# The opening of a decoder layer, rearranged: three arrival signals for x, statistics by row tile, and a first GLA head that begins with its value projections

## Chip, cores and metric

One core of one Trainium2 chip. The metric is the device time of one execution in microseconds. The kernel before took 2632.35 us (median of three runs, 2630.19 to 2633.02).

## The reference

One layer of a hybrid decoder runs for 256 prompt rows and 8 sample rows, which share all weights (264 columns in the kernel, where activations stand transposed). Only its first part matters here:

```python
h = rmsnorm(x, norm_mix_pre)              # x: 256 + 8 rows of 2048
z = h @ w_in                              # columns: pool, dilated q/k/v, then
gq, gk, gv, gr, ga, gates = ...           # GLA: 4 heads of q 256, k 256, v 512, r 512; ga 16 wide
log_a = log_sigmoid(ga @ gla_w_a2 + gla_b_a) / 16
b = cumsum(log_a, within chunks of 64)
q_t, k_t, k_h = q * exp(b), k * exp(-b), k * exp(b_last - b)
A = tril(q_t @ k_t.T); o = A @ v + q_t @ S     # S: state carried from chunk to chunk
y_gla = rmsnorm(o) * gla_norm * silu(gr)
```

After it come the dilated attention, the pooling branch, the merge, cross-attention and the ConvFFN; the change leaves these alone.

## The kernel before

Every weight matrix is read once, in slots of 128 columns by 2048 rows (1 MB). SP issues a slot's load into one of three raw buffers (`load`). ACT writes a rounded copy `weights_hi` in two halves (`split_hi`), DVE the rest `weights_lo = raw - hi` (`split_lo`). PE multiplies a slot with the activations in 16 blocks of three matmuls of 264 columns (`product`: hi by hi, hi by lo, lo by hi), 48 in all, into bank 0, 1 or 2, and the bank is emptied by ACT or DVE. Semaphores count slots and banks: the split of slot c+3 is made after the product of slot c.

The order of work is the order in which each engine's program is written, with waits on counting semaphores; nothing reorders it. POOL first gives every semaphore its starting credits (`credits`), then makes the identity and other constants. ACT's queue issues 17 loads of parameters, SP's queue the two 1 MB tiles of x (128 rows each) and the 8 sample rows, all under one semaphore `x_loaded`; the first weight load waits for it as well.

When all of x is there (L2142 to L2154 on DVE, L994 to L1000 on ACT) the sums of squares of all rows, one square root and one reciprocal for three columns of statistics, and the scaling follow. PE meanwhile turns the parameter rows and makes the attention bias products (L1553 to L1562). Then PE turns x, 128 columns at a time: three transposes (`turn`, L587) give one column tile of 264. ACT writes its `h_hi` (L1010) and DVE its `h_lo` (L2170), from banks 3 to 7 in turn. From the sixth tile on, each round of three transposes is followed by one block (three matmuls) of the first slot, the one that holds ga (`gate_block`, phase `PH_GA`). The text below calls this a round. Five blocks are left when the last tile is turned.

Then ga goes to SBUF, PE makes eight gate sums (`ga @ gla_w_a2`, L1694, 16 rows deep), DVE adds the bias (L2182), ACT and DVE make the log decay and its running sums for head 0 (`log_decay(0)`), and ACT the exponentials. `gla_head` runs 12 slots per head, in the order q0 q1 k0 k1, v0 to v3, r0 to r3. Between slots PE does the small products of the chunked form: `t_kh` (turn k) after slot 4, `a` (scores) after 5, `t_v` (turn v) after 8, `s0` after 9 and `s1` after 10. Head 0 is written out; heads 1 to 3 are a loop, in which `gla_tail` adds the sample rows' work of the head before. The emptying of the q banks multiplies by the exponentials, so it waits for them; the emptying of the v banks (ACT, L1062) is a copy.

## Time and profile before

| | |
|---|---|
| median of three runs | 2632.35 us (2630.19 to 2633.02) |
| span of the profiled execution, first to last instruction | 2631.0 us |
| mean granted TensorE clock | 0.993 |
| busy: PE, DVE, ACT, POOL | 98%, 61%, 48%, 7% |
| DMA | 530.96 MB, mean 202 GB/s |

The profiled execution's own time is not listed apart from the runs; its span stands 1.35 us under their median. PEclk is the granted TensorE clock as a part of 2.4 GHz: 1.00 is the level of 2.4 GHz, 0.50 that of 1.2 GHz. Idle time stands in brackets behind a row, with what ended it.

### The profile page before, as it was taken

What the parts mean: (1) busy time and instruction counts of PE and PEld (TensorE: products, weight loads), DVE (VectorE), ACT (ScalarE), POOL (GpSimd) and SP (SyncE); (2) the same over time, 40 slices, a digit from 0 to 9 for tenths busy, and PEclk for the clock granted to TensorE, in tenths of its full rate; (3) what the DMA queues carried; (4) which work ended last, traced back from release to release, by engine and by line L of the source; (5) the groups of instructions that cost most, each with busy time, mean ns of one, the idle gap of its engine ahead of it and who ended that gap; (6) DMA issues with size and microseconds to landing.
All of it is one profiled execution on the core that took longest, in us unless ns stands there. A gap on an engine that the chain in (4) does not pass through costs nothing. (4 is left out here: it accounts for less than half of the span.)

```text
span 2631.0 us, 53824 instructions
## 1 busy us (share of the span) xinstructions
PE 2567.6 (98%) x20841; PEld 2479.6 (94%) x20841; DVE 1601.4 (61%) x2439; ACT 1254.7 (48%) x1948; POOL 195.7 (7%) x307
## 2 busy tenths in 40 slices
PE   7999999999999999999999999998999999999997
PEld 5988988999999999999999998987999999999997
DVE  4556565544565556555654656546777765777766
ACT  5455555433444444443444644435554554554553
POOL 1112111000111111100000001500000000000000
PEclk9999999999999999999999999999999999999999
DMA  6688789667888888866666747954566567666563
GB/s 202 207 266 272 240 254 297 176 180 209 238 233 232 233 232 230 222 193 192 168 178 207 207 131 208 310 172 129 160 176 182 156 187 194 184 184 175 162 186 107
DMA packets 855053, 530.96 MB, mean 202 GB/s; under 512 B 13961, under 2 KB 832065, under 8 KB 854135
## 3 DMA queue, kind: packets, MB, share of 16 engines
q1 hardware_dynamic: 822583, 440.07, 60.8%
q0 software_dynamic: 27312, 86.50, 9.5%
q10 hardware_dynamic: 5032, 2.62, 0.4%
q8 instruction: 91, 1.49, 0.2%
q14 instruction: 35, 0.29, 0.0%
HBM read 499.79 MB, written 33.29 MB: 203 GB/s over the span
## 5 line engine op out<-in xcount | busy, mean ns | idle before, releaser
L572 PE MATMUL bank<-h_hi,weights_hi 128*128 128x264 f32 x4624 | 1338.7, 290 | 16.2 <-DVE h_lo L2767 7.0
L545 DVE TENSOR_TENSOR weights_lo<-weights_raw,weights_hi 128x1024 fp32r<-128x1024 f32 x814 | 959.5, 1221 | 611.3 <-ACT weights_hi L537 611.1
L573 PE MATMUL bank<-h_lo,weights_hi 128*128 128x264 f32 x4624 | 1317.9, 285 | 0.0
L574 PE MATMUL bank<-h_hi,weights_lo 128*128 128x264 f32 x4624 | 1316.8, 285 | 0.0
L572 PEld LDWEIGHTS bank<-h_hi,weights_hi 128*128 128x128 f32 x4624 | 877.3, 190 | 41.9 <-issue 24.4
L537 ACT ACTIVATE weights_hi<-weights_raw 128x1024 fp32r<-128x1024 f32 x814 | 813.7, 1050 | 204.3 <-PE bank L574 196.5
L573 PEld LDWEIGHTS bank<-h_lo,weights_hi 128*128 128x128 f32 x4624 | 878.4, 190 | 2.1 <-issue 1.9
L574 PEld LDWEIGHTS bank<-h_hi,weights_lo 128*128 128x128 f32 x4624 | 873.9, 189 | 0.0
L572 PE MATMUL bank<-y_hi,weights_hi 128*128 128x264 f32 x1232 | 351.7, 285 | 5.0 <-DVE weights_lo L545 2.6
L574 PE MATMUL bank<-y_hi,weights_lo 128*128 128x264 f32 x1232 | 350.3, 284 | 0.0
L573 PE MATMUL bank<-y_lo,weights_hi 128*128 128x264 f32 x1232 | 348.8, 283 | 0.0
L572 PEld LDWEIGHTS bank<-y_hi,weights_hi 128*128 128x128 f32 x1232 | 232.1, 188 | 6.0 <-issue 3.0
L574 PEld LDWEIGHTS bank<-y_hi,weights_lo 128*128 128x128 f32 x1232 | 232.3, 189 | 0.0
L573 PEld LDWEIGHTS bank<-y_lo,weights_hi 128*128 128x128 f32 x1232 | 232.2, 189 | 0.0
L1148 ACT ACTIVATE qkv<-bank 128x264 f32<-128x264 f32 x72 | 28.1, 390 | 256.2 <-PE bank L574 252.4
L2797 DVE TENSOR_TENSOR squares<-bank,rstd 128x264 f32<-128x264 f32 x88 | 38.0, 432 | 81.4 <-PE bank L574 76.6
L1148 ACT ACTIVATE y_hi<-ffn_value 128x264 f32 (+1 forms) x44 | 18.7, 425 | 140.3 <-DVE ffn_value L2815 140.3
L572 PE MATMUL bank<-memory_normed_hi,weights_hi 128*128 128x256 f32 x256 | 76.5, 299 | 0.0
L573 PE MATMUL bank<-memory_normed_lo,weights_hi 128*128 128x256 f32 x256 | 72.2, 282 | 0.0
L574 PE MATMUL bank<-memory_normed_hi,weights_lo 128*128 128x256 f32 x256 | 71.7, 280 | 0.0
L1499 ACT ACTIVATE ffn_value<-squares,parameters 128x264 f32<-128x264 f32 x44 | 26.7, 608 | 79.8 <-DVE squares L2797 79.8
L964 POOL DMA_DIRECT2D out_conv_p<-conv_new_rows x1 | 0.8, 781 | 842.0 <-DVE conv_new_rows L2859 842.0
(406 smaller groups left out, 2193.9 us busy)
## 6 DMA issues: line engine op xcount, KB each, us to landing
weights_raw<-in_w_in SPq DMA_DIRECT2D x177, 1024.0 KB, 7.0
weights_raw<-in_w_up SPq DMA_DIRECT2D x88, 1024.0 KB, 5.6
weights_raw<-in_w_down SPq DMA_DIRECT2D x64, 704.0 KB, 4.9
gla_state_sample<-in_state_gla POOLq DMA_DIRECT2D x32, 512.0 KB, 8.5
out_gla_s<-gla_state_sample POOLq DMA_DIRECT2D x32, 512.0 KB, 6.2
weights_raw<-in_w_br_gla SPq DMA_DIRECT2D x16, 1024.0 KB, 6.1
weights_raw<-in_w_mix_out SPq DMA_DIRECT2D x16, 1024.0 KB, 6.2
weights_raw<-in_w_xkv SPq DMA_DIRECT2D x16, 1024.0 KB, 6.7
```

The costliest lines, as they stand in the source:

```text
L537: nc.scalar.activation(w_hi[:, r, half], raw[:, r, half], ACT.Copy).then_inc(hi_ready, 1)
L545: nc.vector.tensor_tensor(w_lo[:, r, half], raw[:, r, half], w_hi[:, r, half].bitcast(F32), ALU.subtract).then_inc(lo_ready, 1)
L572: nc.tensor.matmul(out, wh, xh, start=first and n == 0, stop=False)
L573: nc.tensor.matmul(out, wh, xl, start=False, stop=False)
L574: mm = nc.tensor.matmul(out, wl, xh, start=False, stop=last and n == len(blocks) - 1)
L964: pool.dma_start(A["conv_p"][0, 0].rearrange("r (t p) -> t r p", p=P), newtok[:, 0:2, :]).then_inc(conv_out, 16)
L1148: return nc.scalar.activation(out, in_, ACT.Copy)
L1499: nc.scalar.activation(c, sqr[:, j % 3, :], ACT.Identity, scale=param(PC_CW + 176 + col, n), bias=param(PC_CB + col, n)).then_inc(S(f"c{j} ...
L2797: nc.vector.tensor_tensor(u, bank[p.outs[j]][:, 0:T], rstd[:, :], ALU.mult).then_inc(evac[p.outs[j]], 1)
```

## The change

- SP loads the sample rows first, then the two tiles of x, each under its own semaphore; nine small parameter loads and w_a2 move from ACT's queue to SP's, behind x. ACT's queue begins with the bias inputs.
- POOL gives credits to the four setup counters first and clears the statistics before it makes the identity; the other credits come behind the constants.
- The statistics go by part: sample rows, first tile, second tile (its two column halves squared by ACT and DVE side by side). The second tile is scaled in four quarters, and the turning may begin after the first of them. The parameter copy moves from DVE to ACT.
- PE makes the bias products before it turns the parameters.
- From the tenth round on each round has a second block, of slot v0 of head 0. Head 0 runs v0 to v3, q0 q1 k0 k1, r0 to r3 (`FIRST_HEAD`): four gate sums before slot v1 and four behind it, `t_kh` after the ninth slot, `a` and `t_v` after the tenth, `s0` after the eleventh, `s1` after the twelfth. Heads 1 to 3 keep their order (`HEAD`).

The core of the diff (a line of "..." where lines are left out):

```diff
+        QK = [("q", 0), ("q", 1), ("k", 0), ("k", 1)]
+        VS = [("v", t) for t in range(4)]
+        RS = [("r", t) for t in range(4)]
+        class HeadOrder:
+            def __init__(self, kinds, t_kh, a, qx, t_v, s0, s1, o0, o1):
+                self.kinds, self.t_kh, self.a, self.qx, self.t_v = kinds, t_kh, a, qx, t_v
+                self.s0, self.s1, self.o0, self.o1 = s0, s1, o0, o1
+                self.at = {kind: j for j, kind in enumerate(kinds)}
+        HEAD = HeadOrder(QK + VS + RS, t_kh=4, a=5, qx=6, t_v=8, s0=9, s1=10, o0=10, o1=11)
+        FIRST_HEAD = HeadOrder(VS + QK + RS, t_kh=8, a=9, qx=9, t_v=9, s0=10, s1=11, o0=11, o1=11)
+        FIRST_SPLITS = [2, 7, 12]
...
@@ -623,17 +647,25 @@
         @block.sync
         def _(sp):
+            sp.dma_start(xtok_s[:, :], A["x_sample"][:, 0, :]).then_inc(xs_loaded, 16)
             for m in range(2):
-                sp.dma_start(xtok[:, m, :], A["x_prompt"][0, m * P:(m + 1) * P, :]).then_inc(x_loaded, 16)
-            sp.dma_start(xtok_s[:, :], A["x_sample"][:, 0, :]).then_inc(x_loaded, 16)
-            sp.wait_ge(x_loaded, 48)
+                sp.dma_start(xtok[:, m, :], A["x_prompt"][0, m * P:(m + 1) * P, :]).then_inc(x_loaded[m], 16)
+            for name, r0 in PARAMS:
+                src = A[name].rearrange("l (t p) -> (l t) p", p=P)
+                sp.dma_start(prow[r0:r0 + src.shape[0], 0, :], src).then_inc(par_loaded, 16)
+            sp.dma_start(w_a2[:, :], A["gla_w_a2"][0]).then_inc(a2_loaded, 16)
+            sp.wait_ge(x_loaded[0], 16)
+            sp.wait_ge(x_loaded[1], 16)
             load(sp, PH_GA, 0, 0, w_cols(COL_GA))
-            with sp.Fori(0, 4) as h:
-                for j in range(12):
-                    kind, t = [("q", 0), ("q", 1), ("k", 0), ("k", 1)][j] if j < 4 else ("vr"[j // 8], j % 4)
+            def gla_loads(h, order):
+                for j, (kind, t) in enumerate(order.kinds):
                     col = {"q": h * 256 + COL_GQ, "k": h * 256 + COL_GK, "v": h * 512 + COL_GV,
                            "r": h * 512 + COL_GR}[kind]
                     load(sp, PH_GLA, j, h, w_cols(col + t * P))
+            gla_loads(0, FIRST_HEAD)
+            with sp.Fori(1, 4) as h:
+                gla_loads(h, HEAD)
...
-            for s, n in credits:
+            for s, n in first_credits:
                 pool.sem_inc(s, n)
+            nc.gpsimd.memset(stat[:, 0:13], 1.0).then_inc(G_SET("stat1"), 1)
+            nc.gpsimd.memset(stat[:, 13:14], D * EPS).then_inc(G_SET("stat"), 1)
...
-            nc.gpsimd.memset(stat[:, :], 1.0).then_inc(G_SET("stat"), 1)
+            for s, n in credits:
+                pool.sem_inc(s, n)
             nc.gpsimd.memset(scan_keep[:, :], 1.0).then_inc(G_SET("keep1"), 1)
             pool.wait_ge(*G_SET.at("keep1"))
@@ -969,48 +1004,46 @@
         @block.scalar
...
-            act.wait_ge(x_loaded, 48)
+            act.wait_ge(xs_loaded, 16)
             act.wait_ge(*G_SET.at("stat"))
-            ours = ((0, xtok[:, 0, :], P), (2, xtok_s[:, :], NS))
-            for m, x, n in ours:
-                if m:
-                    act.wait_ge(*A_SET.at("sq0"))
-                nc.scalar.activation(junk[0][0:n, :], x, ACT.Square, accum_out=stat[0:n, m:m + 1])\
-                    .then_inc(A_SET(f"sq{m}"), 1)
-            act.wait_ge(*V_SET.at("var"))
-            nc.scalar.activation(stat[:, 6:9], stat[:, 3:6], ACT.Sqrt).then_inc(A_SET("root"), 1)
-            act.wait_ge(*V_SET.at("rstd"))
-            for m, x, n in ours:
-                nc.scalar.activation(x, x, ACT.Copy, scale=stat[0:n, 9 + m:10 + m]).then_inc(A_SET(f"sx{m}"), 1)
+            nc.scalar.activation(junk[0][0:NS, :], xtok_s[:, :], ACT.Square, accum_out=stat[0:NS, 2:3])\
+                .then_inc(A_SET("sq2"), 1)
+            act.wait_ge(*V_SET.at("var2"))
+            nc.scalar.activation(stat[:, 8:9], stat[:, 5:6], ACT.Sqrt).then_inc(A_SET("root2"), 1)
+            act.wait_ge(x_loaded[0], 16)
+            act.wait_ge(*A_SET.at("sq2"))
+            nc.scalar.activation(junk[0][:, :], xtok[:, 0, :], ACT.Square, accum_out=stat[:, 0:1]).then_inc(A_SET("sq0"), 1)
+            act.wait_ge(*V_SET.at("var0"))
+            nc.scalar.activation(stat[:, 6:7], stat[:, 3:4], ACT.Sqrt).then_inc(A_SET("root0"), 1)
+            act.wait_ge(x_loaded[1], 16)
+            act.wait_ge(*A_SET.at("sq0"))
+            nc.scalar.activation(junk[0][:, 0:D // 2], xtok[:, 1, 0:D // 2], ACT.Square, accum_out=stat[:, 12:13])\
+                .then_inc(A_SET("sq1"), 1)
+            act.wait_ge(*V_SET.at("ss1"))
+            nc.scalar.activation(stat[:, 7:8], stat[:, 4:5], ACT.Sqrt, scale=1.0 / D).then_inc(A_SET("root1"), 1)
+            act.wait_ge(*P_SET.at("par"))
+            nc.scalar.activation(par[:, 0:PC_END], bank[6][:, 0:PC_END], ACT.Copy).then_inc(A_SET("par"), 1)
+            act.wait_ge(*A_SET.at("par"))
...
+            def gla_head(h, order, tail):
+                p = PH_GLA
+                if order is HEAD:
+                    decays(h)
+                for j, (kind, t) in enumerate(order.kinds):
+                    if order is FIRST_HEAD and j == 1:
+                        log_decay(0)
+                    if order is FIRST_HEAD and j == 2:
+                        act.wait_ge(*G_PRE.at("at0"))
+                        act.wait_ge(*G_SET.at("rows0"))
+                        act.wait_ge(bias_stored, 32)
+                        act.wait_ge(*V_PRE.at("scan1"))
+                        decays(0)
...
+            def value_block(j, n):
+                if n == 0:
+                    pe.wait_ge(*V_SET.at(f"tz{j + 1}"))
+                return product(pe, PH_GLA, j, j, 0, [H_BLOCKS[n]], first=n == 0, fresh=n == 0, last=n == KB - 1)
+            LAG_G, LAG_V = 5, 9
+            for t in range(KB + LAG_V):
+                if t < KB:
+                    if t == 0:
+                        pe.wait_ge(*V_SET.at("sx2"))
+                        pe.wait_ge(*V_SET.at("sx0"))
+                    if t % 4 == 0:
+                        pe.wait_ge(*V_SET.at(f"sx1_{t // 4}"))
+                    if t == 3:
+                        pe.wait_ge(*A_SET.at("par"))
+                    if t == 4:
+                        pe.wait_ge(*V_SET.at("sb"))
+                    if t > 4:
+                        pe.wait_ge(*V_SET.at(f"lo{t - 5}"))
+                    out = bank[3 + t % 5]
+                    turn(out[:, 0:P], xtok[:, 0, t * P:t * P + P], P)
+                    turn(out[:, P:NP], xtok[:, 1, t * P:t * P + P], P)
+                    turn(out[:, NP:T], xtok_s[:, t * P:t * P + P], NS).then_inc(P_SET(f"x{t}"), 1)
+                if LAG_G <= t < KB + LAG_G:
+                    mm = gate_block(t - LAG_G)
+                    if t == KB + LAG_G - 1:
+                        mm.then_inc(projected, 1)
+                if t >= LAG_V:
+                    mm = value_block(0, t - LAG_V)
             mm.then_inc(projected, 1)
-            def gla_head(h, tail):
+            def gate_sums(tiles):
+                for t in tiles:
+                    if t == 0:
+                        pe.wait_ge(*PH_GA.saved(0))
+                        pe.wait_ge(a2_loaded, 16)
+                        pe.wait_ge(*V_SET.at("sel"))
+                    if t >= 4:
+                        pe.wait_ge(*V_PRE.at(f"z{t - 4}"))
+                    nc.tensor.matmul(bank[3 + t % 4][:, 0:T], w_a2[:, t * P:t * P + P], ga[:, :], start=True, stop=True)\
+                        .then_inc(P_PRE(f"z{t}"), 1)
+            def gla_head(h, order, tail):
                 p = PH_GLA
                 for j in range(12):
-                    product(pe, p, j, j, h, H_BLOCKS).then_inc(projected, 1)
+                    if order is HEAD or j > 1:
+                        product(pe, p, j, j, h, H_BLOCKS).then_inc(projected, 1)
+                    if order is FIRST_HEAD and j == 1:
+                        gate_sums(range(0, 4))
+                        for n in range(KB):
+                            mm = value_block(1, n)
+                        mm.then_inc(projected, 1)
+                        gate_sums(range(4, 8))
...
+            dve.wait_ge(*A_SET.at("sq2"))
+            nc.vector.tensor_scalar(stat[:, 5:6], stat[:, 2:3], 1.0 / D, EPS, ALU.mult, ALU.add).then_inc(V_SET("var2"), 1)
+            dve.wait_ge(*A_SET.at("root2"))
+            nc.vector.reciprocal(stat[:, 11:12], stat[:, 8:9]).then_inc(V_SET("rstd2"), 1)
+            dve.wait_ge(*V_SET.at("rstd2"))
+            nc.vector.tensor_scalar(xtok_s[:, :], xtok_s[:, :], stat[0:NS, 11:12], None, ALU.mult).then_inc(V_SET("sx2"), 1)
+            dve.wait_ge(*A_SET.at("sq0"))
+            nc.vector.tensor_scalar(stat[:, 3:4], stat[:, 0:1], 1.0 / D, EPS, ALU.mult, ALU.add).then_inc(V_SET("var0"), 1)
+            dve.wait_ge(*A_SET.at("root0"))
+            nc.vector.reciprocal(stat[:, 9:10], stat[:, 6:7]).then_inc(V_SET("rstd0"), 1)
+            dve.wait_ge(*V_SET.at("rstd0"))
+            nc.vector.tensor_scalar(xtok[:, 0, :], xtok[:, 0, :], stat[:, 9:10], None, ALU.mult).then_inc(V_SET("sx0"), 1)
+            dve.wait_ge(x_loaded[1], 16)
+            late = xtok[:, 1, D // 2:D]
+            nc.vector.tensor_tensor_reduce(out=junk[1][:, 0:D // 2], in0=late, in1=late, scale=1.0, scalar=0.0,
                                            op0=ALU.mult, op1=ALU.add, accum_out=stat[:, 1:2]).then_inc(V_SET("sq1"), 1)
             dve.wait_ge(*V_SET.at("sq1"))
-            dve.wait_ge(*A_SET.at("sq2"))
-            nc.vector.tensor_scalar(stat[:, 3:6], stat[:, 0:3], 1.0 / D, EPS, ALU.mult, ALU.add).then_inc(V_SET("var"), 1)
-            dve.wait_ge(*A_SET.at("root"))
-            nc.vector.reciprocal(stat[:, 9:12], stat[:, 6:9]).then_inc(V_SET("rstd"), 1)
-            dve.wait_ge(*V_SET.at("rstd"))
-            nc.vector.tensor_scalar(xtok[:, 1, :], xtok[:, 1, :], stat[:, 10:11], None, ALU.mult).then_inc(V_SET("sx1"), 1)
-            dve.wait_ge(*P_SET.at("par"))
-            nc.vector.tensor_copy(par[:, 0:PC_END], bank[7][:, 0:PC_END]).then_inc(V_SET("par"), 1)
+            dve.wait_ge(*A_SET.at("sq1"))
+            nc.vector.scalar_tensor_tensor(out=stat[:, 4:5], in0=stat[:, 1:2], scalar=stat[:, 12:13], in1=stat[:, 13:14],
+                                           op0=ALU.add, op1=ALU.add).then_inc(V_SET("ss1"), 1)
+            dve.wait_ge(*A_SET.at("root1"))
+            nc.vector.reciprocal(stat[:, 10:11], stat[:, 7:8]).then_inc(V_SET("rstd1"), 1)
+            dve.wait_ge(*V_SET.at("rstd1"))
+            for c in range(4):
+                x = xtok[:, 1, c * 512:c * 512 + 512]
+                nc.vector.tensor_scalar(x, x, stat[:, 10:11], None, ALU.mult).then_inc(V_SET(f"sx1_{c}"), 1)
...
+                    if order is FIRST_HEAD and j == 0:
+                        gate_sums(range(0, 4))
                     dve.wait_ge(projected, p.c(j, h) + 1)
-                    if j == 0:
+                    if order is FIRST_HEAD and j == 1:
+                        log_decay(0)
+                        gate_sums(range(4, 8))
```

PE in the tenth round, before (bank 7 takes the turned tile, bank 0 the ga product; names with numbers):

```order
L587 MATMUL bank7<-identity_58,x_tokens_70 128x128 x2
L587 MATMUL bank7<-identity_58,x_tokens_sample_71 128x8
L572 MATMUL bank0<-h_hi_52,weights_hi_50 128x264
L573 MATMUL bank0<-h_lo_53,weights_hi_50 128x264
L574 MATMUL bank0<-h_hi_52,weights_lo_51 128x264
L587 MATMUL bank3<-identity_58,x_tokens_70 128x128 x2
```

and in the change:

```order
L611 MATMUL bank7<-identity_58,x_tokens_70 128x128 x2
L611 MATMUL bank7<-identity_58,x_tokens_sample_71 128x8
L596 MATMUL bank0<-h_hi_52,weights_hi_50 128x264
L597 MATMUL bank0<-h_lo_53,weights_hi_50 128x264
L598 MATMUL bank0<-h_hi_52,weights_lo_51 128x264
L596 MATMUL bank1<-h_hi_52,weights_hi_50 128x264
L597 MATMUL bank1<-h_lo_53,weights_hi_50 128x264
L598 MATMUL bank1<-h_hi_52,weights_lo_51 128x264
L611 MATMUL bank3<-identity_58,x_tokens_70 128x128 x2
```

Three matmuls of slot v0 (bank 1) now stand in the round, ahead of the next tile's transposes.

PE around the gate sums, before (one row for all eight sums):

```order
L573 MATMUL bank<-h_lo,weights_hi 128x264
L574 MATMUL bank<-h_hi,weights_lo 128x264
L1694 MATMUL bank<-gate_low_rank,w_a_67 128x264 x8
L572 MATMUL bank<-h_hi,weights_hi 128x264
L573 MATMUL bank<-h_lo,weights_hi 128x264
```

and in the change, the first four (bank 1 is slot v0, bank 2 slot v1):

```order
L597 MATMUL bank1<-h_lo_53,weights_hi_50 128x264
L598 MATMUL bank1<-h_hi_52,weights_lo_51 128x264
L1655 MATMUL bank3<-gate_low_rank_68,w_a2_67 128x264
L1655 MATMUL bank4<-gate_low_rank_68,w_a2_67 128x264
L1655 MATMUL bank5<-gate_low_rank_68,w_a2_67 128x264
L1655 MATMUL bank6<-gate_low_rank_68,w_a2_67 128x264
L596 MATMUL bank2<-h_hi_52,weights_hi_50 128x264
L597 MATMUL bank2<-h_lo_53,weights_hi_50 128x264
```

The sums stand behind v0 instead of behind the ga slot, and the other four behind v1, each set between full products.

ACT from its last setup DMA to the first h_hi, before:

```order
L986 DMA w_a_67<-in_gla_w_a 16x1024
L994 ACT_TABLE_LOAD
L994 ACTIVATE squares_unread_a,row_stats<-x_tokens 128x2048
L994 ACTIVATE squares_unread_a,row_stats<-x_tokens_sample 8x2048
L997 ACT_TABLE_LOAD
L997 ACTIVATE row_stats<-row_stats 128x3
L1000 ACTIVATE x_tokens<-x_tokens,row_stats 128x2048
L1000 ACTIVATE x_tokens_sample<-x_tokens_sample,row_stats 8x2048
```

and in the change:

```order
L1014 DMA parameter_rows<-in_conv_b 88x128
L1018 ACT_TABLE_LOAD
L1018 ACTIVATE squares_unread_a,row_stats<-x_tokens_sample 8x2048
L1021 ACT_TABLE_LOAD
L1021 ACTIVATE row_stats<-row_stats 128x1
L1024 ACTIVATE squares_unread_a,row_stats<-x_tokens 128x2048
L1026 ACTIVATE row_stats<-row_stats 128x1
L1029 ACTIVATE squares_unread_a,row_stats<-x_tokens 128x1024
L1032 ACTIVATE row_stats<-row_stats 128x1
L1034 ACTIVATE parameters<-bank 128x496
```

ACT's two scalings (L1000) are gone; a square of half a tile, two more square roots and the parameter copy have come in.

## Rows read from the trace of the kernel before

**Rows 1.** The page, part 1: busy time of each engine over the span.
```profile
PE 2567.6 (98%) x20841; PEld 2479.6 (94%) x20841; DVE 1601.4 (61%) x2439; ACT 1254.7 (48%) x1948; POOL 195.7 (7%) x307
```
**Rows 2.** Busy time by stretch, PE: stretch, length, PE busy (count), PEclk, DMA share, GB/s.
```profile
40.00:46.00 6.00, 5.61 (x24) 1.00 0.64 189
...
50.00:59.00 9.00, 9.00 (x32) 0.50 0.44 120
60.00:70.00 10.00, 10.00 (x85) 1.00 0.28 78
```
**Rows 3.** Timeline, 0 to 21 us: start, duration, engine, line, operation, [idle before <-releaser].
```profile
8.92 0.44 ACTq L986 DMA_DIRECT2D w_a<-in_gla_w_a  x1
...
9.45 1.28 ACT L994 ACT_TABLE_LOAD   x1 [9.45 <-POOL gla_q_apart L800]
...
10.71 2.29 DVE L2146 CUSTOM_DVE_ANT_0 squares_unread_b<-x_tokens 128x2048 f32<-128x2048 f32 x1 [10.71 <-DMA x_tokens_sample<-in_x_sample]
10.75 1.91 ACT L994 ACTIVATE squares_unread_a<-x_tokens 128x2048 f32<-128x2048 f32 x1
12.56 0.18 ACT L994 ACTIVATION_READ_ACCUMULATOR squares_unread_a<-x_tokens 128x1 f32 x1
...
14.80 1.28 ACT L997 ACT_TABLE_LOAD   x1
...
16.10 0.21 ACT L997 ACTIVATE row_stats<-row_stats 128x3 f32<-128x3 f32 x1
...
16.55 1.29 DVE L2154 TENSOR_SCALAR x_tokens<-x_tokens,row_stats 128x2048 f32<-128x2048 f32 x1
...
20.49 0.69 PE L587 MATMUL bank<-identity,x_tokens 128*128 128x128 f32 x2 [1.51 <-ACT x_tokens_sample L1000]
```
**Rows 4.** DMA of 4 to 5 us (SP queue: packets, MB, share).
```profile
q1 hardware_dynamic: 50, 0.41, 96.6%
```
**Rows 5.** DMA of 8 to 9 us, SP queue; then of 10 to 11 us (issue, last number us to landing).
```profile
q1 hardware_dynamic: 33, 0.11, 31.6%
...
weights_raw<-in_w_in SPq DMA_DIRECT2D x1, 1024.0 KB, 5.7
```
**Rows 6.** Timeline of PE, 25 to 43 us: the rounds and the matmuls behind them.
```profile
25.41 0.59 PE L572 MATMUL bank<-h_hi,weights_hi 128*128 128x264 f32 x1
...
41.28 0.59 PE L572 MATMUL bank<-h_hi,weights_hi 128*128 128x264 f32 x1
...
42.11 0.42 PE L572 MATMUL bank<-h_hi,weights_hi 128*128 128x264 f32 x1
42.33 0.42 PE L573 MATMUL bank<-h_lo,weights_hi 128*128 128x264 f32 x1
```
**Rows 7.** Timeline of PE, 46 to 60 us: the gate sums and head 0's first product.
```profile
46.08 2.07 PE L1694 MATMUL bank<-gate_low_rank,w_a 16*128 16x264 f32 x8 [0.47 <-ACT gate_low_rank L1018]
...
49.89 3.88 PE L1694 MATMUL bank<-gate_low_rank,w_a 16*128 16x264 f32 x8 [1.75 <-DVE gla_log_decay L2182]
53.71 0.59 PE L572 MATMUL bank<-h_hi,weights_hi 128*128 128x264 f32 x1
...
59.81 0.29 PE L572 MATMUL bank<-h_hi,weights_hi 128*128 128x264 f32 x1
```
**Rows 8.** Timeline of DVE: the first steps after head 0's second and third product.
```profile
68.36 0.17 DVE L2212 TENSOR_SCALAR gla_q_sample<-bank 128x8 f32<-128x8 f32 x1 [2.23 <-PE bank L574]
...
74.17 0.29 DVE L2221 TENSOR_TENSOR gla_k_even_to_end<-bank,gla_k_even_to_end 128x128 f32<-128x128 f32 x1 [2.23 <-PE bank L574]
```
**Rows 9.** Timeline of ACT: the decay exponentials of head 0, first and last.
```profile
57.66 1.28 ACT L1049 ACT_TABLE_LOAD   x1 [2.83 <-DVE gla_log_decay L2195]
...
61.92 0.20 ACT L1058 ACTIVATE gla_chunk_decay<-gla_log_decay 128x8 f32<-128x8 f32 x1
```
**Rows 10.** Timeline of PE in head 1: the first two sample products.
```profile
148.95 1.03 PE L1671 MATMUL bank<-gla_state_sample,gla_q_apart 128*8 128x512 f32 x4 [0.57 <-DVE gla_state_sample L2278]
150.20 1.03 PE L1671 MATMUL bank<-gla_state_sample,gla_q_apart 128*8 128x512 f32 x4 [0.21 <-DVE gla_state_sample L2278]
```

More of the change, by code:

```diff
@@ L510, in build @@
         sp_turns = sem("sp_turns")
-        x_loaded = sem("x_loaded")
+        x_loaded = [sem(f"x_tile{m}_loaded") for m in range(2)]
+        xs_loaded = sem("x_sample_loaded")
         par_loaded = sem("parameters_loaded")
@@ L1594, in gla_head @@
                     tail(j)
-                    if j == 4:
+                    if j == order.t_kh:
                         pe.wait_ge(*V_GLA.at("ke1_1", h))
@@ L2247, in gla_head @@
                     tail(j)
-                    if j == 4:
+                    if j == order.t_kh:
                         dve.wait_ge(*P_GLA.at("t_kh", h))
```

179 lines of the change are left out of this document (71 added, 108 removed).

## Prediction

> **What bounds the kernel now.** I read the page's busy times first: PE is busy for 98% of the span [rows 1], so time can be won only where PE stands idle or runs slowly. The busy times by stretch say where. From 60 us on PE starts 85 matmuls per 10 us at a granted clock of 1.00, the 2.4 GHz level; from 50 to 59 us it starts 32 in 9 us at 0.50, the 1.2 GHz level; from 40 to 46 us the view prints 1.00, yet only 24 start in 6 us [rows 2]. The timeline corrects that print: at 42.11 and 42.33 us two neighbouring matmuls stand 0.22 us apart [rows 6], while a product of 48 matmuls at full speed takes 5.81 us, 0.121 each (DVE begins on the second product's result at 68.36 and on the third's at 74.17 us [rows 8]). So PE works at the lower level almost from its first instruction, and the record's 1.00 ahead of the first fall isn't to be believed.
>
> The opening in order of time: everything waits for all of x until 10.71 us, then a chain of ACT and DVE work runs until PE can turn x at 20.49 us [rows 3]. The first gate block follows at 25.41 us, the sixteenth tile's block, the last one in a round, at 41.28 us: ten rounds of 1.59 us [rows 6]. The gate sums come in two sets: four from 46.08 us, which take 2.07 us, the other four from 49.89 us after 1.75 us of idling for DVE, and these take 3.88 us. The first product of head 0 starts at 53.71 us, and full speed is there at 59.81 us [rows 7]. Everything up to 74.1 us (the end of the third product) is the stage in which this change is worth something; behind it PE is the bound, and an earlier start is kept.
>
> **The change, step by step.** I follow PE to the end of its third head 0 product, which both versions have behind the same transposes, ga product and eight sums.
>
> *1. Until the turning starts.* ACT's DMA issues end at 9.36 us in the trace (the last one is 0.44 us long [rows 3]); the change leaves 7 of 17, which from the first at about 1 us on gives 4.5 us. Then on ACT, all by [rows 3]: table load 1.28, square of the sample rows 1.91 + 0.18 (the square takes its columns' time, however few the rows), table load 1.28, root 0.21: 9.4 us. Square of the first tile 2.09: 11.5. Two scalar steps between DVE and ACT, estimated at 0.5 with their hand-overs: 12.0. DVE scales the first tile, 0.2 + 1.29: 13.5, and squares half of the second, half of 2.29 with its read-out: 14.7. ACT's own half (about 1.1) is done by 13.2. Three scalar steps, 0.7: 15.4. A quarter of the second tile, a quarter of 1.29: 15.8. So PE turns its first tile at 15.8 instead of 20.49 us, 4.7 us earlier.
>
> What must be there by then: the first tile by 9.4, the second by 12.0. The SP queue moves 0.41 MB per us [rows 4], the last 0.11 MB of x pass between 8 and 9 us [rows 5], and the release at 10.71 [rows 3] shows a lag of some 2 us. One tile is 1.05 MB, so the first, now behind 64 KB of sample rows, lands at about 8. ACT's bias inputs, 0.19 MB, now run beside it and cost half a microsecond. The bounds: no delay, or both tiles landing only at 11.7, 2.3 us late. I take no delay, since the bytes of the first tile are through by 6.
>
> Covered: the nine parameter loads and w_a2, now issued by SP behind x, wait for nothing and land near 12 us; the turning of the parameters, which needs them, comes behind the bias products and has until 15.8. Should they be late, each microsecond goes straight to PE. POOL's credits come later by its few constants, but the first weight load, which needs them, still waits for x. The parameter copy on ACT sits in ACT's wait for the first tile.
>
> *2. The rounds.* The first gate block follows 4.92 us behind the first transposes [rows 3, 6]: 20.7. The first slot, issued about half a microsecond later than before and 5.7 us to landing [rows 5], is there by 17; its split stands behind the third tile's place in ACT's program. Four more rounds at 1.59 bring PE to the tenth tile's gate block at 27.1. From there a round has three more matmuls, 3 x 0.22, so 2.25 us: the sixteenth tile's gate block is at 40.6. ACT and DVE need about 0.5 us each per round, and a lag of five rounds covers the slot splits.
>
> *3. The dense part.* Behind that point stand 48 matmuls (six of each in pairs, the rest of v0 alone). Before, PE ran densely from 41.28 and was at full speed by 46.08, when four sums took 2.07 us (the other four took 3.88 at 0.50), so at most 4.8 us later; the second time it took 53.71 to 59.81, 6.1 us [rows 6, 7]. I take 5.0: 23 matmuls at 0.22, until 45.6, and 25 at 0.121. v0 ends at 48.6 us.
>
> *4. Sums and products.* ga leaves its bank while PE still finishes v0, so the 0.47 us of waiting [rows 7] goes. Four sums 2.07, v1 5.8, four sums 2.07, v2 5.8: 64.4 us. DVE adds the first bias terms during v1, so the 1.75 us go as well. Before, the same point was 74.1: **9.7 us won**. The 9.7 are 4.7 of earlier start, and the rest is idling and cold matmuls.
>
> *5. The rest of head 0.* The decay exponentials took 4.5 us on ACT, table load to last one [rows 9]. They now start when DVE has scanned after v1, at about 59, and are ready by 64; the first q product ends at 76. That cover is 12 us; without it the bank of q0 would stay full. What is late next is k1: DVE's long log decay of heads 1 to 3 now stands between k0 and k1, and by my count k1's result is ready for `t_kh` 0.6 us before PE asks, since r0 lies between. The small products are the same ones. Head 0 now ends with `s1`, which PE does while ACT makes head 1's exponentials; before, these held up the first two sample products of head 1 by 0.57 and 0.21 us [rows 10]. Bounds: 0 and 0.78; I take 0.78, as ACT starts them over a microsecond earlier against the product.
>
> Sum: 9.7 + 0.8 = 10.5 us off the profiled span of 2631.0, 2620.5; the median of the runs stands 1.35 above that span, so **2622 us**.
>
> **Rivals.**
>
> *Full speed comes already in the rounds.* From the tenth round on PE's work is denser than before. If the clock rises at about 31 us, five rounds shrink to some 1.25 us (six matmuls at 0.121, transposes at half their time) and the dense part to 5.8: v0 ends near 42 instead of 48.6, and the time is 2615. Against it: from 25.41 to 41.28 us the old rounds followed one behind the other, and the matmuls after them still stood 0.22 us apart [rows 6]. For it: the new rounds hold six matmuls where the old held three. The Trainium skill, "TensorE: Matmul & The Clock Gate", section "What's actually happening", says that the throttled clock is the default and that activity releases it; by that rule alone a PE that is never idle from 15.8 us on would rise early. The trace qualifies it: a PE counted as busy isn't enough. Chance 0.2.
>
> *x doesn't come tile by tile.* If both tiles land together at 11.7, step 1 loses 2.3 us: 2624. For it: only the joint release at 10.71 is on record [rows 3]. The Trainium skill, "DMA: Bandwidth & Descriptors", section "Queues, rings and completion order", says that a later descriptor may finish before an earlier one, and that an engine takes turns between queues; no row here shows either. Chance 0.1.
>
> *The clock falls in the sums.* Before, it fell soon after the first set of sums: those and the idling behind them are all that PE did from 46.08 to 49.89, and the next matmuls ran at 0.50 [rows 2, 7]. Now full products stand on both sides, and there is no idling. If it falls all the same, behind each set, v1 and v2 each run some 27 matmuls at 0.22 and lose 2.7 us: 2627. Chance 0.08.
>
> *Slower than before.* The same weakness, from one point on: if the clock has not risen when v0 ends, the sums come before any rise. All of v0 cold ends at 51.2, sums 3.88, v1 at 0.22 throughout 10.6, sums 3.88, then v2 with a start like that of 53.71, whose product ended two products ahead of 74.1 (8.8): 78.4 against 74.1, less 0.8: 3.5 us slower, 2636; with a rise that comes later still, in v3, 5 us more. What decides is whether the 48 dense matmuls, 10.6 us at the lower level, suffice for the rise; before, 4.8 and 6.1 us did. Chance 0.06.
>
> **How the numbers follow.** The main case has 0.56: 2622, by itself 2619 to 2624.5 (start of turning a microsecond either way, rise of the clock at 4 to 6.1 us, the 0.78 won or not, k1 late by little). A measurement of this kernel can tell about 0.2%, 5.3 us, from no change, so faster means under 2627.1. The main case, the early rise and late x are all faster, 0.86, of which I take off 0.02 for what no row shows in the new order of head 0; a fall in the sums lies at the boundary and goes to "same" for the most part, with part of the slower rival. That gives 0.85 faster, 0.11 same, 0.04 slower. The range takes in the early rise below and the fall in the sums above: 2614 to 2627.
>
> **What would show it.** Right: the first transposes of x near 15.8 us; matmuls of v0 in the rounds; no idle time on PE between the last round and v2; the third product's end near 64.4; no row of idling for the first two sample products of head 1; everything behind merely earlier. Wrong: ACT waiting for x's first tile beyond 9.4 us; matmul spacing of 0.12 in the rounds (better) or of 0.22 in v1 or v2 (worse); PE waiting for `ke1_1`, for the parameters or for DVE's gate terms; the clock's fall in the granted row behind either set of sums.

## The result and the profile after

The changed kernel takes **2621.44 us** (median of 4 runs, 2619.3 to 2621.83) against 2632.26 us before (median of 4): ratio 0.995, 95% interval 0.9939 to 0.9962 (the two medians alone give 0.996). The forecast was 2622 us. The profiled execution of after took 2619.3 us, its span is 2617.8; before's span was 2631.0, so 13.2 us lie between the two traces where the sum had 10.5. It is the fastest of the four executions of after; the spans of the other three are 2619.7 to 2620.3, so the medians lie only 10.8 us apart. The total was met by luck as well as by the sum: the clock rose earlier than the main case had it, a part of that lead was given back 1600 us later, and the other three executions took some 2 us more than the one that was traced. Two executions below stood in a much slower state (2807.91 us of before_again, 6427.83 us of warm) and are left out of all medians.

Part 1 of the page after, against [rows 1]:

```profile
PE 2560.7 (98%) x20841; PEld 2474.6 (95%) x20841; DVE 1601.9 (61%) x2447; ACT 1252.2 (48%) x1951; POOL 195.1 (7%) x308
```

The instruction count of TensorE is the same; it is busy 6.9 us less, which is the net of products that became warm (run at the 2.4 GHz level) and of others that became cold (at 1.2 GHz). The other 6.3 us of the 13.2 are idling that went.

The timeline of after, 12 to 17 us, answers to [rows 3]:

```profile
11.86 1.29 DVE L2221 TENSOR_SCALAR x_tokens<-x_tokens,row_stats 128x2048 f32<-128x2048 f32 x1
...
12.35 1.06 ACT L1029 ACTIVATE squares_unread_a<-x_tokens 128x1024 f32<-128x1024 f32 x1 [0.72 <-DMA x_tokens<-in_x_prompt]
...
14.97 1.06 PE L611 MATMUL bank<-identity,parameter_rows 128*128 128x128 f32 x5 [2.21 <-DMA parameter_rows<-in_gla_b_a]
15.01 1.68 DVE L2235 TENSOR_SCALAR x_tokens<-x_tokens,row_stats 128x512 f32<-128x512 f32 x4
...
15.82 0.63 PE L611 MATMUL bank<-identity,x_tokens 128*128 128x128 f32 x2
```

The first turn of x stands at 15.82, before at 20.49. But its queue is another than the one reckoned with: TensorE waited 2.21 us for the parameters, which landed near 14.97 instead of 12, and x stood behind their five turns. VectorE's first quarter of the second tile was ready at about 15.4 (15.01 and a quarter of 1.68), so by estimate the parameters cost some 0.4 us. The second tile held ScalarE until 12.35.

TensorE in the rounds of after, against [rows 6]:

```profile
27.04 0.59 PE L596 MATMUL bank<-h_hi,weights_hi 128*128 128x264 f32 x1
...
28.31 0.42 PE L598 MATMUL bank<-h_hi,weights_lo 128*128 128x264 f32 x1
28.53 0.63 PE L611 MATMUL bank<-identity,x_tokens 128*128 128x128 f32 x2
...
29.29 0.39 PE L596 MATMUL bank<-h_hi,weights_hi 128*128 128x264 f32 x1
29.51 0.28 PE L597 MATMUL bank<-h_lo,weights_hi 128*128 128x264 f32 x1
...
35.78 0.39 PE L596 MATMUL bank<-h_hi,weights_hi 128*128 128x264 f32 x1
...
41.62 0.28 PE L598 MATMUL bank<-h_hi,weights_lo 128*128 128x264 f32 x1
41.83 2.04 PE L1655 MATMUL bank<-gate_low_rank,w_a 16*128 16x264 f32 x8
43.80 0.39 PE L596 MATMUL bank<-h_hi,weights_hi 128*128 128x264 f32 x1
```

The first round with six products begins at 27.04; in the second, from 29.3 us on, a product of 264 columns takes 0.28 us instead of 0.42. The rounds shrink from 2.25 to 1.30 us, and v0 ends at 41.7 us. Both sets of sums take 2.04 us (before 2.07 and 3.88, [rows 7]), and the third product ends at 57.7 instead of 74.1. The stretches of [rows 2], after:

```profile
40.00:46.00 6.00, 6.00 (x42) 1.00 0.79 234
50.00:59.00 9.00, 9.00 (x67) 1.00 0.42 114
60.00:70.00 10.00, 10.00 (x85) 1.00 0.74 201
```

In head 1 the idle time ahead of the first two sample products [rows 10] has no row any more; heads 2 and 3 keep theirs (0.57 and 0.21 us), as the loop has it. The idle rows are not the whole of it: from the last product ahead of these sample products to the first behind them it took 3.06 us before (148.10 to 151.16) and takes 1.88 us now (131.79 to 133.67), so 1.2 us are won there.

```profile
131.79 0.28 PE L598 MATMUL bank<-h_hi,weights_lo 128*128 128x264 f32 x1
132.01 1.73 PE L1746 MATMUL bank<-gla_state_sample,gla_q_apart 128*8 128x512 f32 x8
133.67 0.39 PE L596 MATMUL bank<-h_hi,weights_hi 128*128 128x264 f32 x1
```

From there on the lead is constant, 17.4 to 17.5 us. One transfer serves as a mark through this text: SyncE's load of one weight tile of w_xkv (the sixth tile behind the query weights, 1 MB), issued at 1650.85 us before and at 1633.43 after, 17.42 us earlier. At the end 13.2 us are left. The 4.2 us go in the cross-attention that follows. There, in the timeline of after:

```profile
1651.60 2.00 ACT L561 ACTIVATE weights_hi<-weights_raw 128x1024 fp32r<-128x1024 f32 x2 [1.81 <-DMA weights_raw<-in_w_xkv]
...
1661.12 1.12 PE L611 MATMUL bank<-identity,x_probs 128*128 128x128 f32 x4 [1.15 <-DVE x_probs L2770]
1661.89 0.56 PE L596 MATMUL bank<-memory_normed_hi,weights_hi 128*128 128x256 f32 x1
1662.25 0.41 PE L597 MATMUL bank<-memory_normed_lo,weights_hi 128*128 128x256 f32 x1
...
1680.31 0.66 PE L611 MATMUL bank<-identity,x_probs 128*128 128x128 f32 x4 [0.63 <-DVE x_probs L2770]
```

and TensorE in two stretches of it (columns as in [rows 2]):

```profile
1660.00:1670.00 10.00, 8.88 (x62) 0.83 1.07 300
1680.00:1690.00 10.00, 9.69 (x86) 0.83 0.76 235
```

ScalarE waits 1.81 us for that tile, VectorE's split of it comes later, the softmax behind the split too, TensorE stands idle for x_probs twice, and behind each wait its products take 0.41 us again: 1.78 us of waiting and 2 x 1.7 us for a clock of 0.83 in 10 us, 5.2 us at most, since some of the waiting lies in the slow stretches. Before's trace lost 0.6 us in this stage and no clock: there ScalarE waited 1.17 us, for the tile behind this one, and TensorE once, 0.58 us.

```profile
1677.32 2.01 ACT L537 ACTIVATE weights_hi<-weights_raw 128x1024 fp32r<-128x1024 f32 x2 [1.17 <-DMA weights_raw<-in_w_xkv]
...
1684.29 0.38 PE L587 MATMUL bank<-identity,x_scores_sample_slots 128*8 128x128 f32 x2 [0.58 <-DVE xq_sample_tokens_lo L2675]
```

That leaves 4.6 for a difference of 4.2. The tile itself, in the DMA view of the 0.1 us in which it was issued, last number us to landing: before

```profile
weights_raw<-in_w_xkv SPq DMA_DIRECT2D x1, 1024.0 KB, 13.4
```

and after

```profile
weights_raw<-in_w_xkv SPq DMA_DIRECT2D x1, 1024.0 KB, 18.1
```

It shares the DMA engines with 24 loads of the key and value caches (256 KB each), which GpSimd issues one behind the other. ScalarE came to it at 1649.79 us (1651.60 less the wait of 1.81), 16.4 us after its issue: what lands later than that is waited for.

### The profile page after: what moved, and what is told of

Its sections match the earlier page's. It is cut to its first block and busy times, and to the rows that moved or that the text cites. A ratio compares the mean times of both kernels' runs of the same rounds, so it can differ in the third digit from the quotient of the medians.

```text
span 2617.8 us, 53803 instructions
## 1 busy us (share of the span) xinstructions
PE 2560.7 (98%) x20841; PEld 2474.6 (95%) x20841; DVE 1601.9 (61%) x2447; ACT 1252.2 (48%) x1951; POOL 195.1 (7%) x308
```

## The experiments

Two questions: which part of the change makes the clock rise in the rounds, and whether the loss in the cross-attention belongs to the change. All marks come from the traces (one each); ratios are those of the runs against the kernel before on the same chip, and the experiments ran on three chips. "Full speed" is the first product of 264 columns under 0.3 us, or sums of 2.04 to 2.07 us; "third ends" is the start of the last matmul of head 0's third product. A lead is how much earlier than in the first trace of before TensorE does the same instruction, or the tile is issued.

```
kernel              x turned  full speed  third ends  tile issued  landing  span    ratio (95%)
before              20.49     46.08       73.84       1650.85      13.4     2631.0
before_again        20.32     44.35       72.68       1649.65      19.1     2635.0  1.0    (0.999 to 1.0011)
before_cache_later  20.51     46.10       73.57       1650.57      13.3     2630.5  0.9994 (0.9986 to 1.0003)
opening_only        15.71     41.35       68.99       1646.02      15.4     2628.6  0.9985 (0.9975 to 0.9995)
order_only          20.48     40.62       64.78       1640.68      15.9     2621.9  0.997  (0.9959 to 0.9982)
v0_behind           15.69     38.42       61.27       1636.92      18.9     2622.2  0.9961 (0.9948 to 0.9974)
after               15.82     29.51       57.57       1633.43      18.1     2617.8  0.995  (0.9939 to 0.9962)
after_again         15.80     31.89       58.65       1636.08      21.1     2623.6  0.9951 (0.9938 to 0.9964)
cache_later         15.79     33.71       59.16       1634.85      16.5     2616.4  0.9934 (0.9921 to 0.9947)
cache_later_again   15.62     33.87       59.33       1635.18      13.5     2615.2  0.9932 (0.9919 to 0.9946)
warm                15.88     29.53       57.61       1633.51      18.8     2617.1  0.9945 (0.9932 to 0.9958)
warm_gap            15.53     30.33       57.92       1635.24      16.2     2615.3  0.993  (0.9917 to 0.9944)
warm_all            16.17     21.71       55.48       1632.74      16.5     2612.8  0.9925 (0.9911 to 0.9938)
```

**The changed kernel again** (no edit).

> The changed kernel unaltered, for a second trace. Theory A (the six matmuls of a round lift the clock): full speed again within the rounds, between 27 and 34 us, v0 done near 42 us. Theory B (the early rise was a matter of the moment): full speed anywhere between 29 and 46 us, v0 done between 42 and 49 us. On the later part: if what was given back in the cross-attention (17.5 us ahead in head 1, 13.2 at the end) belongs to the change, it is given back again, by 3 to 5 us; if it is chance, the loss differs by some us from trace to trace. Time 2618 to 2623 us.

Median 2620.04 us. The rise came at 31.9 us, in the rounds again. The lead is 16.4 us in head 1; 1.5 us of it go near 1315 us, where the clock falls for a short time, which leaves 14.8 at the tile; 7.4 are left at the end. ScalarE waited 4.83 us for the tile. How much is given back differs from run to run.

**v0 behind the rounds**: three products in each round, v0's sixteen blocks behind the gate product.

```diff
-            LAG_G, LAG_V = 5, 9
+            LAG_G, LAG_V = 5, 21
```

> The blocks of v0 leave the rounds and stand behind the ga product; all else is the changed kernel. Theory A: the rounds stay at 1.59 us and at 0.22 us per matmul to their end near 37 us, full speed comes about 5 us later, v0 is done near 47 us, 5 us later than in the changed kernel, and the time is about 5 us longer, 2626 us. Theory B: full speed comes at 29 us all the same, v0 is done near 42 us, and the time is that of the changed kernel, 2621 us.

2623.66 us. The rounds stayed cold to the end, and the clock rose behind them:

```profile
37.80 0.42 PE L598 MATMUL bank<-h_hi,weights_lo 128*128 128x264 f32 x1
...
38.42 0.28 PE L598 MATMUL bank<-h_hi,weights_lo 128*128 128x264 f32 x1
```

So the three products more in a round are what lets it rise in them. The third product came 3.7 us later than in after (61.27 against 57.57); by the runs the intervals of the two ratios overlap.

**The opening alone**: head 0 and its sums in the old order.

```diff
-            for t in range(KB + LAG_V):
+            for t in range(KB + LAG_G):
...
-                if t >= LAG_V:
-                    mm = value_block(0, t - LAG_V)
-            mm.then_inc(projected, 1)
...
-            gla_head(0, FIRST_HEAD, lambda k: None)
+            gate_sums(range(8))
+            gla_head(0, HEAD, lambda k: None)
```

> The opening of the change (signals, statistics by part, bias products ahead) with the old order behind it: no v0 in the rounds, eight gate sums behind the ga product, head 0 as the other heads. If the parts add up: turning starts at 15.8 instead of 20.5 us, the idling at the gate sums stays, third product of head 0 done 4.7 us earlier than before, time 2627.5 us. If the clock's rise before the sums fails with the new start, up to 2 us less is won: 2629.5 us.

2629.54 us. The turns came 4.8 us earlier, and 4.85 us of lead at the third product is all that comes of it; 2.5 are left at the end (0.8 went in the cross-attention, 1.5 near 1830 us, where the clock fell for a short time). The pattern of [rows 7] is there again, earlier:

```profile
41.35 2.04 PE L1656 MATMUL bank<-gate_low_rank,w_a 16*128 16x264 f32 x8 [0.47 <-ACT gate_low_rank L1050]
45.16 3.88 PE L1656 MATMUL bank<-gate_low_rank,w_a 16*128 16x264 f32 x8 [1.77 <-DVE gla_log_decay L2264]
48.98 0.59 PE L595 MATMUL bank<-h_hi,weights_hi 128*128 128x264 f32 x1
```

**The order alone**: old loads, statistics and bias products; v0 in the rounds, the sums around v1.

```diff
-            act.wait_ge(xs_loaded, 16)
+            act.wait_ge(x_loaded, 48)
...
-            act.wait_ge(x_loaded[0], 16)
...
-            act.wait_ge(x_loaded[1], 16)
```

> The old opening (all of x under one signal, statistics at once, parameters turned first), with the new order from the tenth round on: v0 in the rounds, sums around v1, values first in head 0. Theory A: full speed within the rounds, near 34 us; head 1 reached 12.8 us earlier than before (17.5 less 4.7); time 2620 us, or 2623.5 us if 4 us are given back in the cross-attention. Theory B or an early start as the condition of the early rise: full speed only near 50 us, head 1 reached 6 us earlier, time 2626 us.

2624.38 us; 10.2 us of lead at the tile. Full speed came at 40.6 us, within the rounds of six products, which began at 31.75: later than theory A had it (34) and earlier than theory B (50). The order is worth twice the opening; 4.85 and 10.25 make 15.1 of the 16.4 and 17.5 us that the two traces of the whole change have in head 1, which leaves 1.3 to 2.4 us for the moment at which the clock happens to rise or an effect of both together; one trace each can't part these.

**The kernel before again** (no edit).

> The kernel before, unchanged, for a second trace of it. Theory 'chance': how long the sixth weight tile of w_xkv behind the queries takes to land among the cache loads differs from run to run (13.4 us in the first trace of before, 15.4 to 21.1 in the five traces of changed kernels), so this trace has it anywhere from 13 to 21 us, and ScalarE waits up to 5 us for it. Rival 'belongs to the change': 13 to 14 us again and a ScalarE wait of about 1 us there, as in the first trace. Under both the time is 2630 to 2634 us, its ratio to before 1.000 within 0.001.

2635.58 us, ratio 1.0. The same tile took 19.1 us this time, and this trace lost 5.2 us from the tile to the end: 1.2 us ahead of the first trace at the tile, 4.0 behind it at the end. Of the 5.2, 3.7 went in the cross-attention, 1.5 behind it. So the kernel before can lose as much there, and "belongs to the change" falls. This was another chip, and its execution one of the slower ones (2636.71); how often the kernel before loses it is not shown. TensorE's waits in 1600 to 1720 us of this trace:

```profile
PE bank L587 <- DVE x_probs L2687: 2.5, 2, 1.8
```

**The third key cache behind the late tile's split**: 16 cache loads in a row instead of 24.

```diff
-            for h in (1, 2):
-                for half in range(2):
-                    cache_load("k", h, half)
+            for half in range(2):
+                cache_load("k", 1, half)
...
             key_rows(0)
+            pool.wait_ge(hi_ready, 2 * PH_KB.c(5) + 2)
+            for half in range(2):
+                cache_load("k", 2, half)
```

> The changed kernel with the eight loads of the third key cache (k of head 2) on GpSimd's queue put behind the split of that late weight tile; nothing is left out. Theory 'late weight': the cache loads make the weight tile late, the late split on VectorE makes the softmax late, and TensorE's waits for it drop its clock. With 16 instead of 24 cache loads in a row the tile lands within 13 us, ScalarE's wait for it and TensorE's waits for x_probs fall under 0.5 us in all, the granted clock of 1660 to 1690 us is 1.00, and the lead over before, 16 to 17.5 us in head 1, is still over 15 us at the end: 2614 to 2618 us, ratio 0.993 to 0.994. Rival 'belongs to the stage': the 4 to 7 us are lost all the same, 2619 to 2622 us.

2617.93 us. The tile took 16.5 us, more than the 13 expected, but ScalarE, which comes to it 16.4 us after its issue here too, waits only 0.2 us. The wait of TensorE that was the second one in after stays (0.64 us), the first one is gone, and the clock holds:

```profile
1660.00:1670.00 10.00, 10.00 (x79) 1.00 1.06 334
1680.00:1690.00 10.00, 10.00 (x103) 1.00 1.00 298
```

16.0 us of lead at the tile, 14.6 at the end; the 1.4 us that went are lost behind the cross-attention. The kernel before with the same shift:

> The kernel before with the same shift of the third key cache's loads. Theory 'late weight': the trace of before lost only 0.6 us of TensorE's time to this (a wait of 0.58 us) and no clock, so at most 1 to 2 us come back: 2630 to 2632.5 us, ratio 0.9990 to 1.0005. If before's runs lose in this place as much as the changed kernel's do, 2626 to 2629 us.

2632.54 us, ratio 0.9994: no difference that can be told, so no sign that the kernel before loses much here in most executions. In its trace the tile took 13.3 us, and nothing was lost (0.3 us of lead at the tile, 0.5 at the end). The shift a second time in the changed kernel:

> The changed kernel with the third key cache's loads behind the late weight tile, a second time, beside the two kernels built on it. Theory 'late weight': again no loss in the cross-attention (TensorE's waits for x_probs under 1 us in all, granted clock 1.00 from 1660 to 1690 us), 2616 to 2620 us, ratio 0.993 to 0.9945. If the first result was luck, TensorE waits 2 us or more there and the clock falls, 2620 us or more.

2616.76 us; nothing lost (15.7 and 15.8 us of lead). In all four traces of the new kernels that had the shift, TensorE waited 0.6 to 0.7 us in this stage and kept its clock. Of the six without it, after, after_again, v0_behind and warm lost 3.5 to 7.3 us in the cross-attention, and the two that hold a part of the change lost little (opening_only 0.8, order_only 0.1). The landing parts them. Measured against the first trace of before, on matching TensorE instructions from the tile's issue to 1800 us: in the eight traces whose tile landed within 16.5 us at most 0.8 us went there, in the five with 18.1 us or more 3.5 to 7.3. So theory "late weight" holds for what the lateness costs. That the shift makes the tile land in time is not as sure: it did so in all five traces with the shift, and in three of the eight without. By the medians the shift gives 2 to 5 us; the ratios' intervals overlap, so that size is not settled.

**Products of the identity in TensorE's idle time**, to see whether the clock can be up before the rounds.

```diff
+            def warm(count):
+                for _ in range(count):
+                    nc.tensor.matmul(bank[5][:, 0:P], ident[:, :], ident[:, :], start=True, stop=True)
+            pe.wait_ge(*G_SET.at("ident"))
+            warm(12)
             pe.wait_ge(bias_loaded, 32)
...
+            warm(6)
             pe.wait_ge(par_loaded, 14 * 16)
```

> The changed kernel with 18 products of the identity with itself (128 columns each, written to a bank that nobody reads before it is overwritten) on TensorE in its two idle stretches of the opening, 12 ahead of the bias products and 6 ahead of the parameter turns; work is added, none left out. Theory 'density': what TensorE does decides when its clock rises, so the rise comes before the first turns, the rounds run at full speed from 15.8 us, bounded by the splits on ScalarE and VectorE, and the first value product ends at 37 to 39.5 us instead of 41.6 to 42.7: lead in head 1 of 19 to 21 us, time 2616 to 2619.5 us. Rival 'the rounds alone': the thin rounds from 16 to 27 us let it fall again and it rises at 29 to 32 us as before, no gain: 2619.5 to 2622 us. If the added products make the bias products late, the first turn comes later than 15.8 us.

2621.53 us, no gain: the third product stands at 57.61, as in after. The clock did rise, and was lost again (each product is two matmuls in the count):

```profile
2.23 4.28 PE L1587 MATMUL bank<-identity 128*128 128x128 f32 x24 [2.23 <-POOL identity L823]
7.41 2.10 PE L1593 MATMUL bank<-onehot,rel_bias_rows 33*8 33x383 f32 x6 [0.90 <-DMA rel_bias_rows<-in_rel_bias]
...
14.46 0.65 PE L611 MATMUL bank<-identity,parameter_rows 128*128 128x128 f32 x5 [2.73 <-DMA parameter_rows<-in_gla_b_a]
15.88 0.66 PE L611 MATMUL bank<-identity,x_tokens 128*128 128x128 f32 x2 [0.77 <-DVE x_tokens L2240]
```

The bias products of 383 columns took 2.10 us where after's took 4.00; then 2.73 us passed without work, and the turns of x were cold. The next two kernels (both with the cache shift) ask whether the idle stretch did that, or the rounds. Here the idle stretches ahead of the turns are filled:

```diff
-            warm(12)
+            warm(15)
...
-            warm(6)
+            warm(15)
...
             mm.then_inc(P_SET("par"), 1)
+            warm(2)
```

> The kernel with the third key cache's loads shifted, and 32 products of the identity with itself that fill all three idle stretches of TensorE ahead of the first turn (15 ahead of the bias products, 15 ahead of the parameter turns, 2 behind these); work is added, none left out. In the kernel with 18 of them the clock rose at 5 us and fell at 15.3 us, behind 2.73 us without work, and rose again only at 29 us. Theory 'the idle stretch': the fall came from the stretch without work, so here the clock stays up through the rounds, and the first value product ends at 37.5 to 39.5 us; 2613 to 2616 us. Theory 'thin rounds': the turns and the three-product rounds can't hold it, it falls between 16 and 26 us and rises at 29 to 33 us, first value product at 41.5 to 43.5 us; the same time as without the products, 2616 to 2620 us.

2616.74 us. The turns of x now start at full speed, at 15.53 us. They run ahead of the other engines, so that TensorE waits 0.83 and 0.96 us, and the clock falls in the second of these waits, at 20.0 us, ahead of the first block; the rounds of three products behind it stay at the lower level:

```profile
18.50 0.41 PE L611 MATMUL bank<-identity,x_tokens 128*128 128x128 f32 x2 [0.83 <-DVE sample_bias_all L2248]
...
20.54 0.56 PE L596 MATMUL bank<-h_hi,weights_hi 128*128 128x264 f32 x1 [0.96 <-DVE weights_lo L2253]
20.90 0.42 PE L597 MATMUL bank<-h_lo,weights_hi 128*128 128x264 f32 x1
```

And here the first nine rounds have such products too:

```diff
+                    if t < LAG_V:
+                        warm(2 if t < LAG_G else 1, out[:, 0:P])
                     turn(out[:, 0:P], xtok[:, 0, t * P:t * P + P], P)
```

> The same with 14 more of these products in the first nine rounds (two in each of the first five, one in each of the next four, ahead of the turns and into the bank that the turns then overwrite); work is added, none left out. Theory 'the idle stretch': no better than with the gaps alone, up to 1 us later for the products in rounds 5 to 8. Theory 'thin rounds': with the rounds filled the clock stays up from 5 us on, the first value product ends at 38 to 40 us, lead in head 1 of 18.5 to 20.5 us instead of 15 to 17.5: 2613 to 2616 us. If neither holds, the clock falls in the rounds all the same and the products make them longer: 2618 to 2622 us.

**2615.3 us**, the fastest kernel here. The first gate block and all that follows, up to 1311 us, runs at full speed:

```profile
21.48 0.39 PE L596 MATMUL bank<-h_hi,weights_hi 128*128 128x264 f32 x1
21.71 0.28 PE L597 MATMUL bank<-h_lo,weights_hi 128*128 128x264 f32 x1
...
21.95 0.39 PE L1589 MATMUL bank<-identity 128*128 128x128 f32 x2
```

Third product at 55.48; 19.6 us of lead in head 1, 18.1 at the tile and at the end (1.5 went near 1313 us, where the clock fell for a short time). Filling the idle time ahead of the turns was not enough, filling the rounds was, as "thin rounds" had it. But warm_gap still had idle time among the turns, and here the added products take that too; whether little work or those waits let the clock fall is not parted. Against cache_later the medians differ by 2.6 and 1.5 us, the intervals overlap.

## Why the prediction was right, and where it was not

- **Step 1, the start**: 15.8 forecast, 15.82 measured, for a reason only partly named. "Land near 12 us", said of the parameters, failed: 14.97. The cover it was given ("has until 15.8") did not suffice, since the turning that follows takes time too; that cost some 0.4 us, and x was ready as much earlier (15.4). The tiles of x did come one by one; that rival falls.
- **Step 2, the rounds**: first gate block 20.7 forecast, 20.73 measured; the tenth tile's 27.1 and 27.04. The last six rounds failed with step 3.
- **Step 3, the clock**: "I take 5.0 ... until 45.6 ... v0 ends at 48.6 us" is the step that failed. It counted the time to the rise from the end of the rounds; the clock rose at 29.3, within them (31.9 in the second trace), and v0 ended at 41.7. The rival of full speed in the rounds had this (v0 near 42, chance 0.2). The old rounds were no evidence against it: they hold three products, and v0_behind shows that such rounds stay cold while rounds of six don't.
- **Step 4, sums and products**: 9.7 us by sums of 2.07 and products of 5.8 us after v0; both sizes held nearly (2.04 and 6.0), and there was no idle time and no fall of the clock. With step 3 mended, 16.4 us are won at the third product, 6.7 more than forecast.
- **Step 5**: forecast 0.78 us at head 1's first sample products, measured 1.2; the idle rows that it went by show only a part. k1 caused no wait.
- **"The rest merely earlier"** failed by 4.2 us. It holds from head 1 to 1633 us to within 0.1 us. Then one weight tile landed 4.7 us later than in the trace that the sum was made against. That trace was a mild case: the kernel before loses 3.7 us there in another execution. The early rise was worth 6.7 us more than forecast, the cross-attention took 4.2 of it back, and the median of after lies 3.6 us above the traced span where the sum had 1.35. So the total came out at 2621.4.
- **Slower**: what decides was named as whether the clock has risen when v0 ends. It had, in every trace with v0 in the rounds.

What stays open: why the tile's landing ranges from 13.3 to 21.1 us, and whether the changed kernel draws a late one more often. Without the shift, its four traces with the opening and the new order had 18.1 to 21.1, and the others 13.4, 19.1, 15.4 and 15.9. Open too is why the clock falls for a short time near 1315 us in some traces (after_again, warm_gap, warm_all) and once more between 1814 and 1836 us in others (before_again, opening_only, v0_behind, cache_later), each time at a cost of some 1.5 us.

## What to carry to other kernels

Put full products into the thin rounds of an opening rather than behind them: here TensorE's clock then rose there, and the products behind them ran at full speed; check by the duration of one product shape. A lead won early has to pass every stage that loads much at once: look in the trace of before for a wait there that is just covered (here 1.17 us on ScalarE for a weight tile of w_xkv, and for the tile ahead of it a landing after 13.4 us, when ScalarE came to it after 16.3), and take the bulk loads out of its way. Take a second trace of the kernel before, since a stage that costs 0.6 us in one execution may cost some 4 us in the next.

## What was not expected of the hardware

- Without any idle time TensorE stood at either level. In 24 to 28 us of after it is busy 4.00 of 4.00 us, with 16 matmuls, nearly all of them in rounds of three products, and all at the lower level; in 29 to 33 us, with six products in a round, the clock is up:

```profile
24.00:28.00 4.00, 4.00 (x16) 1.00 1.20 291
29.00:33.00 4.00, 4.00 (x28) 1.00 1.05 400
```

The rounds of three stayed at 1.2 GHz in all traces but warm_all, which reached them at 2.4 and had added products in them; warm_gap had 2.4 GHz in the turns ahead of them and lost it there, at 20.0 us, with idle times of 0.83 and 0.96 us. The Trainium skill, "TensorE: Matmul & The Clock Gate", section "What's actually happening", has activity release the throttle; the runs agree in so far as the clock rose in the rounds with more products and not in the thin ones, and a busy 4.00 of 4.00 us in the view did not tell the two apart.

- The granted clock stands at 1.00 in the first of these rows although products of 264 columns take 0.42 us: ahead of the first recorded change the column tells nothing, the duration of a known shape does.
- From the start of the denser stretch to the rise it took 2 us (after, 27.04 to 29.2) to 8 us (order_only, 31.75 to 39.8), so a forecast of one value, 5.0 us, was too sharp.
- The late tile was overtaken: issued at 1633.43, it landed 18.1 us later, while the eight loads of mem_cache_c that GpSimd issued behind it took 8.6 us in the median. The Trainium skill, "DMA: Bandwidth & Descriptors", section "Queues, rings and completion order", has each DMA engine take turns between queues; the trace is in line with it, with 60.5% of the engines' time on GpSimd's queue and 40.6% on SyncE's in 1633.4 to 1641.1 us, but does not show the turns themselves.
